# Modulation part 4 on GpSimd, and two weight blocks moved in VectorE's order, in a two-block transformer kernel

## The reference, cut to what matters

```python
mod = c @ w_ada[l] + b_ada[l]                       # 1024 -> 6 * 1024
shift_m, scale_m, gate_m, shift_f, scale_f, gate_f = jnp.split(mod, 6, axis=-1)
h = modulate(rms_norm(x, g_pre_mix[l]), shift_m, scale_m)
proj = h @ w_in[l]                                  # q, k, v, gates g_a and g_m, ...
...
merged = sigmoid(g_a) * (y_a @ w_branch_attn[l]) + sigmoid(g_m) * (y_m @ w_branch_mlstm[l])
mix = merged @ w_out[l]
x = x + gate_m[:, None, :] * rms_norm(mix, g_post_mix[l])
h2 = modulate(rms_norm(x, g_pre_ffn[l]), shift_f, scale_f)
...
```

## Time and profile before

| | us |
|---|---|
| median of 3 runs | 841.0 (839.71 to 841.39) |
| the profiled execution, its time | 842.11 |
| its span, first to last instruction | 840.3 |
| TensorE busy | 784.3 (93%) |
| VectorE busy | 643.9 (77%) |
| ScalarE busy | 390.6 (46%) |
| GpSimd busy | 18.5 (2%) |

### The profile page before, as it was taken

The page is one execution under the profiler, slowest core; times in us unless marked ns, Lnnn a source line. Parts: engine busy times, 40 slices in busy tenths (PEclk is TensorE's granted clock), DMA queues, the critical chain, the costliest instruction groups (busy, mean ns, idle before and its releaser), DMA issues.

```text
span 840.3 us, 16562 instructions
## 1 busy us (share of the span) xinstructions
PE 784.3 (93%) x6962; PEld 717.1 (85%) x6962; DVE 643.9 (77%) x849; ACT 390.6 (46%) x547; POOL 18.5 (2%) x40
## 2 busy tenths in 40 slices
PE   2979998998899999999998999989998999999996
PEld 2878998998778899999887987789967999999874
DVE  5858988898876887877877899887378778555456
ACT  3447753664364444444334884521233544454350
POOL 0200000000001000000001000000010000000000
PEclk9989999999999999999999999999999999999998
DMA  9795576682565999988983644520125669665521
GB/s 359 244 332 170 181 258 219 217 285 76 158 219 183 347 314 309 317 280 301 343 293 100 222 146 127 188 90 4 29 70 184 199 206 347 209 196 196 200 100 51
DMA packets 96024, 173.73 MB, mean 207 GB/s; under 512 B 7767, under 2 KB 55230, under 8 KB 95950
## 3 DMA queue, kind: packets, MB, share of 16 engines
q1 hardware_dynamic: 92848, 165.87, 59.1%
q0 software_dynamic: 1872, 5.86, 2.2%
q10 hardware_dynamic: 1230, 0.95, 0.3%
HBM read 171.60 MB, written 1.05 MB: 205 GB/s over the span
## 4 chain that ended last, share of the span: by engine, by line
PE 67%; DVE 19%; ACT 5%; issue 3%; DMA 3%; ACTq 1%; DVEq 0%; SPq 0%; POOL 0%; POOLq 0%
PE bank L2052 12%; PE bank L2054 12%; PE bank L2053 12%; PE bank L2315 4%; PE bank L2316 4%; PE bank L2317 4%; DVE wlo L441 3%; PE bank L2486 3%; DVE acc L468 3%; PE bank L2027 2%; PE bank L2028 2%; PE bank L2029 2%; DVE arena L468 1%; ACT whi L609 1%; DMA raw<-in_w_in 1%
## 5 line engine op out<-in xcount | busy, mean ns | idle before, releaser
L609 ACT ACTIVATE whi<-raw 128x1024 fp32r<-128x1024 f32 (+2 forms) x220 | 225.8, 1036 | 256.8 <-PE bank L2054 99.0
L441 DVE TENSOR_TENSOR wlo<-raw,whi 128x1024 fp32r<-128x1024 f32 (+2 forms) x220 | 259.9, 1195 | 88.2 <-ACT whi L609 84.2
L2052 PE MATMUL bank<-hh,whi 128*128 128x256 f32 x1016 | 286.1, 282 | 11.7 <-DVE wlo L441 8.7
L2053 PE MATMUL bank<-hl,whi 128*128 128x256 f32 x1016 | 283.3, 279 | 0.0
L2054 PE MATMUL bank<-hh,wlo 128*128 128x256 f32 x1016 | 283.3, 279 | 0.0
L2052 PEld LDWEIGHTS bank<-hh,whi 128*128 128x128 f32 x1016 | 192.3, 189 | 15.9 <-DVE wlo L441 7.9
L2053 PEld LDWEIGHTS bank<-hl,whi 128*128 128x128 f32 x1016 | 192.7, 190 | 0.5 <-issue 0.5
L2054 PEld LDWEIGHTS bank<-hh,wlo 128*128 128x128 f32 x1016 | 192.3, 189 | 0.0
L468 DVE SCALAR_TENSOR_TENSOR acc<-raw,cc,acc 128x1024 f32<-128x1024 f32 x70 | 89.7, 1281 | 7.8 <-DMA raw<-in_w_ada 4.2
L2315 PE MATMUL bank<-whi,ffh 128*128 128x512 f32 x168 | 65.9, 392 | 1.1 <-DVE wlo L441 1.1
L2316 PE MATMUL bank<-wlo,ffh 128*128 128x512 f32 x168 | 65.4, 389 | 0.0
(11 more groups left out here) (445 smaller groups left out, 1052.1 us busy)
## 6 DMA issues: line engine op xcount, KB each, us to landing
raw<-in_w_ada SPq DMA_DIRECT2D x96, 512.0 KB, 5.3
raw<-in_w_in SPq DMA_DIRECT2D x54, 512.0 KB, 4.6
raw<-in_w_ffn_in SPq DMA_DIRECT2D x88, 256.0 KB, 3.9
raw<-in_w_ffn_gate SPq DMA_DIRECT2D x44, 256.0 KB, 4.6
raw<-in_w_ffn_up SPq DMA_DIRECT2D x44, 256.0 KB, 5.5
raw<-in_w_ffn_down SPq DMA_DIRECT2D x22, 512.0 KB, 5.7
raw<-in_w_ffn_out SPq DMA_DIRECT2D x22, 512.0 KB, 3.2
raw<-in_w_out SPq DMA_DIRECT2D x16, 512.0 KB, 4.6
```

The costliest lines, as they stand in the source:

```text
L441: eng.tensor_tensor(lo[:, 0:nk * width], raw[:, b % RAW, 0:nk * width], hi[:, 0:nk * width].bitcast(fp), ALU.subtract)\
L609: act.activation(weight_place(g)[0][:, 0:nk * width], raw[:, b % RAW, 0:nk * width], ACT.Copy)\
L2052: mm(o, wh[:, k, c], xh[:, kk_, :], start=first, stop=False)
L2053: mm(o, wh[:, k, c], xl[:, kk_, :], start=False, stop=False)
```

## The change

Part 4's eight blocks (c8 and c9) are scaled and added by GpSimd, with two instructions a block instead of VectorE's one. The bias row is waited for there, since the sum starts on top of it. The ring of loads waits for GpSimd's count for these blocks. c9 moves in the stream from beside wo0 to beside bm1. On VectorE, wo0's first block is prepared before `branch_low(0)`, its second after it, its third between `branch_sum(1)` and `branch_low(1)` and its fourth behind that; TensorE's and ScalarE's programs are the same.

```diff
@@ stream()
     head = ["c0", "c1", "c2", "c3", "o_if", "qm", "km", "vm", "g0", "qa", "kva", "c8", "g1", "c4", "g2", "c5",
-            "g3", "c6", "ba0", "c7", "ba1", "bm0", "bm1", "wo0", "c9", "wo1"]
+            "g3", "c6", "ba0", "c7", "ba1", "bm0", "bm1", "c9", "wo0", "wo1"]
@@ build
-        ready = [("dve", b + 1) for b in range(len(order))]
+
+        ready, made = [], {"dve": 0, "pool": 0}
+        for what, *_ in order:
+            who = "pool" if what in ("c8", "c9") else "dve"
+            made[who] += 1
+            ready.append((who, made[who]))
@@ GpSimd
+            def add_pieces(beside):
+
+                for b in at_block[with_piece(beside)]:
+                    what, i, _, width, _, landed, _ = order[b]
+                    k, (_, count) = 4 * (int(what[1:]) % 2) + i, ready[b]
+                    x, to = raw[:, b % RAW, 0:width], part_acc(4)
+                    pool.wait_ge(sem(f"raw{b % RAW}_in"), landed)
+                    pool.tensor_scalar(x, x, cc[:, 0, k:k + 1], None, ALU.mult).then_inc(sem("piece_scaled"), 1)
+                    pool.wait_ge(sem("piece_scaled"), count)
+                    if count > 1:
+                        pool.wait_ge(sem("pool_blocks"), count - 1)
+                    pool.tensor_tensor(to, to, x, ALU.add).then_inc(sem("pool_blocks"), 1)
+
             gate_bias(4)
+            pool.wait_ge(sem("c_in"), 16)
+            pool.wait_ge(sem("spreads"), 16 * BIAS_AT[4])
+            add_pieces("kva")
+            add_pieces("bm1")
             pool.wait_ge(sem("h_ready"), 8)
@@ VectorE
             branch_sum(0)
+            prepare("wo0", slice(0, 1))
             branch_low(0)
-            prepare("wo0", slice(0, 1))
+            prepare("wo0", slice(1, 2))
             by_gate("bm1", 12)
             branch_sum(1)
-            prepare("wo0", slice(1, 3))
+            prepare("wo0", slice(2, 3))
             branch_low(1)
@@ VectorE
-            prepare("wo0", slice(3, 8))
+            prepare("wo0", slice(3, 4))
             prepare("wo1")
```

## The result

The kernel after takes 852.6 us (median of 4 runs, 852.03 to 855.49) against 841.19 before: ratio 1.0133, interval 1.011 to 1.0156, which is 11.2 us slower (9.3 to 13.1).

The account below looks back on a forecast made before the run. It took TensorE, busy 93% of the span, to bound the kernel. Terms -1.5 + 0 + 1.2 + 1.0 = +0.7 on the median 841.0 gave 841.7 us, no change; range 838.7 to 846.3.

Parts of the forecast that it names:

- Step 4: GpSimd and VectorE hindering each other at SBUF: cost 1.0 us, one stand, with 3.5 as upper bound.
- the first rival: VectorE's two-input instructions wait out GpSimd's scalings and adds, decisive at c9's first block: +3.2 us, 844.2; chance 0.26.
- five places: Tight places where VectorE may stand: where c8's first and last and c9's first, second and last blocks land; about 3.5 us.
- Step 2: Ring slots held by GpSimd: a block takes 3.3 us, at most 4.9, and no load is later: 0.
- a sign of being wrong: The forecast called itself wrong if, among other signs, c8's sum ends behind 120 us.
- Step 3: New order around wo0: first wlo waits for ScalarE, gaps of 2.0 and 2.7, clock falls behind the second: +1.2 us.
- the other branch: Around wo0 the clock falls behind the first gap and slow matmuls fill the second: -0.5 us.
- Step 1: c8 leaves VectorE, so g1's last wlo comes sooner and TensorE's wait goes, reaching the scores: -1.5 us.

Follow-up runs that it names:

- e8: Kernel after with five memsets per block in place of GpSimd's scaling and add: +0.2 us against the kernel before.
- e7: Kernel after without GpSimd's eight scalings, its eight adds kept: +3.4 us against the kernel before.
- g1: Kernel after with three memsets in place of each GpSimd scaling, adds kept: +8.3 us against the kernel before (elsewhere g1 is a weight).
- e5: Kernel after with GpSimd's scalings and adds replaced by empty instructions that only signal: -0.9 us against the kernel before.
- e3: Kernel before with only VectorE's new order around wo0, c9 staying on VectorE beside wo0: +2.5 us against the kernel before.
- f1: e3 with ScalarE splitting wo0's first two blocks before it rounds merged half 0: -0.3 us against the kernel before.

## Why the prediction was wrong

I forecast 841.7 within 838.7 to 846.3, with 0.38 for slower. It is 852.6, past the end of the range. The cause was among the rivals, with a price under a third of its size.

- **Step 4, GpSimd and VectorE (taken 1.0, bound 3.5; measured 12.1): the step that failed.** The mechanism was named, as the first rival and with the Trainium skill (SBUF — State Buffer, "Who interferes with whom"), but the bound was no bound. I took half an add at each of five places and then took slack off. In the trace a step stands for the add's whole rest, up to 2.2, seven short steps are hit by adds and scalings together (8.4 us), and wlo on top; the rotation was not on my list, and the row steps were hit three times. Slack of 0.3 to 1.4 a place was taken off, and at c8's blocks there was none: the row steps end 3.3 later, and TensorE's results for the masks come later with them. The nearest row, the memset, I let pull the value down, although it differed from the added work in the one property in question; e8 shows that such a row says nothing of a read. A bound from above had to be the number of adds (8) by about their length of 2, so 16, before anything is taken off for cover, beside a VectorE that is busy for 86% of 100 to 260 us in the kernel before. By e8 the hold of the slots is about 1 of the 12.1 or nothing.
- **Step 2, the slots (0): about right in price, wrong in its term.** I put a block at 3.3 with 4.9 as upper end; it takes 5.3 at best, a scaling of 2.85 or more and an add of 2.4, so outside both ends. The adds by streams were near (2.9 against 2.4), the scaling was not (2.0 against 3.3 in the mean). c8's sum ended at 127.2 instead of 116.0, past the 120 that was named as a sign of being wrong, and SyncE waited 11.8 us for GpSimd in three waits. Holding a slot for 5.2 costs little all the same (e8). What the length did cost is in step 4: twice the time in which GpSimd reads, and adds that fall 3 us later (e7 against g1).
- **Step 3, the order (1.2): the wait right, the branch right only beside GpSimd's work.** The first wlo waits 2.13 for ScalarE, as worked out. In the kernel after the gaps are 2.6 and 2.6 for a forecast of 2.0 and 2.7, and the low clock, 0.66 in the window behind the second gap, came. But in e5, the same order without GpSimd's arithmetic, the gaps are 1.8 and 1.0, the clock (0.73) falls behind the first, and wo0 takes 0.4 less than before: this is the other branch, worked out as -0.5. e3's +2.5 is no measure of this step, since c9's blocks stand in the way there. That the wait for the split is what the order costs, f1 shows against e3: with the split made first, 2.8 less.
- **Step 1 (-1.5): partly right.** In e5, where nothing hinders VectorE, TensorE's wait of 1.5 before g1's last block is gone (in the kernel after 0.8 of it is left). But its trace is 0.7 early at 94 us for no reason of the change, and g1's last wlo comes 1.4 early: only 0.7 is won there, because the masks, which I took as fixed, wait for TensorE 0.64 and 0.53 on the way. Taking all eight blocks off VectorE for nothing is worth 3.4 us with the new order (e5 against e3, a difference of two comparisons), most of it around wo0, where c9's blocks are gone from VectorE (15.4 us against 18.1); with the old order it was not run.
- **The sum.** -0.9 and 12.1 give the 11.2. The forecast's other terms sum to -0.3, near that -0.9; one term was short by 11.

## What to carry to other kernels

Before work goes to GpSimd beside a busy VectorE, ask of each instruction whether it reads SBUF, the memory on the core in which tiles such as `raw` and `arena` lie. If so, count it as time taken from VectorE, up to its whole length, wherever VectorE's steps are on the chain, and ask where the chain's *short* steps are: one add of 2.4 us stretches a step of 0.16 to 2.41. Writes held no two-input wlo, but one-input steps for up to 0.9 us. And an instruction moved into a gap must have its input by then: here the gap was filled with a wait, until the engine that feeds it was reordered too; with that, c9's last blocks moved behind wo0's, and nothing on GpSimd, the kernel won 4 us.

## What the runs showed of the hardware that I had not expected

- GpSimd's scaling of 128x1024 floats by one number a partition takes longer than its add of two such tiles. The groups of the kernel after, 84 to 262 us:

```profile
L536 POOL TENSOR_SCALAR raw<-raw,cc 128x1024 f32<-128x1024 f32 x8 | 26.5, 3313 | 130.2 <-DMA raw<-in_w_ada 130.2
L540 POOL TENSOR_TENSOR arena<-arena,raw 128x1024 f32<-128x1024 f32 x8 | 19.2, 2399 | 0.7
```

  The Trainium skill (GPSIMD Engine Reference, section 4.1) has one-input instructions at roughly line rate and two-input ones about twice as slow. The order of the two is the other way round here, and the measurement decides. Its measured add (section 3.1), halved to this size as an estimate, is 2.25 and fits the 2.40.
- A scaling, also a read, holds VectorE for about 0.9 us at most, though it lasts 2.85; an add holds it to its end. The held steps on four columns end 1.1 us after the scaling began, in 13 of 14 cases in nine traces (1.4 in the other), as if it held VectorE in its first microsecond alone. The Trainium skill (SBUF — State Buffer, "Who interferes with whom") has the engine that is first, beside VectorE's 2-port modes, hold the shared ports "for the whole instruction"; that fits the add only.
- It is not only two-input steps that stand: L1413 has one tensor input, and stood 2.41 beside an add in e7 and 1.02 beside a memset in e8 (L1419 there). Not every one-input step does: the BATCH_NORM steps inside the add of 208.26 in the kernel after keep their 0.29 and 0.18.
